# One decoder layer on one core: a gate projection is put in front of the SSD scan, the pieces between its half chunks get shorter, and the log gates of the GLA heads get PSUM banks of their own

## The chip, the cores and the metric

One core of a Trainium2 chip runs the whole program. The metric is the device time in microseconds (us); 3 runs of the kernel before are at hand, and one profiled execution.

## The reference

One layer of a decoder for 1024 prompt tokens and 8 samples of 8 tokens (1088 tokens), width 1024, all float32. h = RMSNorm(x) goes through one wide input projection `u = h @ W['w_in']`, whose columns feed three token mixers and the gates of each:

```python
g_log = log_sigmoid(g_low @ W['gla_w_alpha'] + W['gla_b_alpha']) / GLA_TAU      # log gates, 4 heads of 128
o, gla_s_new = gla_chunked(gq, gk, gv, g_log, gla_s)                            # GLA
y, ssd_h_new = ssd_chunked(sx, dt, a, sb, sc, ssd_h)                            # SSD, 16 heads, 2 groups
gates = sigmoid(gate_logits).reshape(b_, l_, 3, D_MODEL)
merged = gates[:, :, 0] * b_lru + gates[:, :, 1] * b_gla + gates[:, :, 2] * b_ssd
x = x + merged @ W['w_mix_out']
```

After it come cross attention and a SwiGLU.

## The kernel before

Activations lie transposed, features on the 128 partitions and tokens along the row. Every float32 product is made of three matmuls in a rounded format: high part by high part, high by low, low by high. A projection of one tile of 128 output features is 3 x 8 = 24 matmuls ("steps") for each of three groups of tokens (384, 384 and 320 columns, `GROUPS`), so 72 for a tile. SyncE loads a weight tile (512 KB) into one of three slots as soon as the tile that was there is used up; GpSimd splits it into Wh and Wl (L710, L712).

`plan()` writes down the order of all results in PSUM. Six banks form a ring, and a name in `OWN_BANK` has a fixed bank. Each bank has two counters: TensorE waits before its first matmul into a bank until the engine that reads the result before it there has let it go (`free_bank`), and a reader waits until the result is ready (`ready`). Each engine works its own list strictly in order.

Stages, in TensorE's order: LRU; four GLA heads; the `gla_out` product; the input projections of SSD (`sx`, `sz`) and their transposes (`st`, `zt`, L850); the SSD scan; the final states of the 8 samples; `ssd_out`; the mix; attention; the feed-forward.

**GLA heads.** `log_gates(h)` (L865) makes `ga{h}:0` to `:2` with one short product a group, ScalarE reads each twice (Abs L1717, Relu L1719), and then come the projections `gq`, `gk`, `gr`, `gv` of head h. For heads 1 to 3 the call stands at the end of the head before, just ahead of `turn_o(TT)`, the transposes of its last output, which wait until VectorE has scaled that output (L2493); it lies in bank 0 (`go{h}_8:0`). After those transposes VectorE multiplies (L2472), ScalarE copies two tiles (L1794), and only then reads `ga{h+1}`. For head 0 ScalarE comes to `ga0` when a store of the stage before has landed. All `ga` take their banks from the ring: 1, 2, 3 for head 0, then 0, 1, 2, then 5, 0, 1, then 4, 5, 0. The first projection `gq` takes 4, 5, 0 for head 0, then 3, 4, 5, then 2, 3, 4, then 1, 2, 3.

**SSD scan.** 8 chunks of 128 tokens by 2 head groups are 16 half chunks q. TensorE's list for one: `sums(q/2+1)` for even q, `products(q)` (L1146, L1149, L1153), the transposes `turn_y(q-1)` (L850), `fill(("q", q, 0))`, `decays(q+2)` (L1129), `fill(("q", q, 1))`. `fill` (L786) runs steps of the gate projections `og2_0` to `og2_7`, for which nobody in the scan waits. All `og2` results lie in bank 5. VectorE's list: `decay_steps(q+2)` (L2607), six operations of `outputs(q)` (L2634 to L2652), in even q `tile_sums`, then `matrices(q+2)` (L2616), `split_y(q-1)`, `scale_y(q)` (L2659). ScalarE's: in even q `exp_sums`, then `hi_y(q-1)` (L1958), `load_z`, `exp_decays(q+2)` (L1941), `load_xs`, `roots_y(q)` (L1950, L1951), and last `copy_gates_by_group(("q", q, 1))`: for each group of 24 steps that ends in that gap it copies bank 5 to a buffer (L1488) and stores it (L1490).

After the projections of SSD, and before it enters the scan, ScalarE waits for the stores of z, then issues the first loads (L1907, L1913); VectorE waits for the first of them, then makes `decay_steps(0)`. TensorE's first `decays(0)` waits for that.

**States.** For each of 8 samples: L1204, L850, L1211, L850, then `fill(("s", b))`. Then `decays` and `products` of the samples' own half chunks 16 and 17, `fill(("s", 8))`, `turn_y` of both, `fill(("s", 9))`. Behind the last gate copy ScalarE starts the loads of `ssd_out`.

Of the kernel before, what the change touches and what calls it, by code (L numbers as in the profile page):

```python
# [20 lines left out]
DT = D // P  # L21
LP = 1024
NB = 8
# [3 lines left out]
TT = LP // P  # L27
GROUPS = [(0, 384), (384, 384), (768, 320)]
# [3 lines left out]
GH, DK, DV, GCH = 4, 128, 256, 64  # L32
# [28 lines left out]
def gap_parts(b, tiles, gaps):  # L61


    parts, steps = {}, 3 * DT
    todo = [(t, g) for t in tiles for g in range(len(GROUPS))]
    at = 0
    for gap, n in gaps:
        parts[gap] = []
        while n:
            m = min(n, steps - at)  # L70
            parts[gap].append((f"og{b}_{todo[0][0]}", *todo[0], at, at + m))
            at, n = at + m, n - m
            if at == steps:
                at = 0
                todo.pop(0)
    assert not todo and at == 0
    return parts
# [3 lines left out]
GAPS = {}  # L81
# [7 lines left out]
OWN_BANK = {}  # L89
# [5 lines left out]
for _b in range(NB):  # L95
# [2 lines left out]
OWN_BANK |= {f"og2_{_t}:{_g}": 5 for _t in range(DT) for _g in range(len(GROUPS))}  # L98
OWN_BANK |= {f"og1_{_t}:{_g}": 4 + (_t * len(GROUPS) + _g) % 2 for _t in range(DT) for _g in range(len(GROUPS))}

GAPS |= gap_parts(2, range(DT), [(("q", _q, _i), 12) for _q in range(2 * TT) for _i in range(2)]
                  + [(("s", _b), 12) for _b in range(NB)] + [(("s", NB), 48), (("s", NB + 1), 48)])

# [4 lines left out]
def plan():  # L110
# [16 lines left out]
    def banks(name, n=len(GROUPS)):  # L127

        jobs.extend(f"{name}:{g}" for g in range(n))
# [66 lines left out]
    for t in range(DT):  # L196
        use([("in", C_Z + t * P)], f"sz{t}")
        banks(f"zt{t - 1}" if t else "qt")
    banks(f"zt{DT - 1}")
    banks("ss0", 2)  # L200
    banks("ss1", 2)
    for q in range(2 * TT):
# [9 lines left out]
    q = 2 * TT  # L212
# [53 lines left out]


WLIST, JOBS = plan()
RING = 6

# [16 lines left out]
def build(nc, ins, outs):  # L287
    I, O = ins, outs
    ctx = ExitStack()
    with ctx:  # L290
# [3 lines left out]
        def sem(name):  # L294
            return ctx.enter_context(nc.semaphore(name))
# [54 lines left out]
        def wk(i, n=WT, off=0):  # L350
            return WK[:, i * WT + off:i * WT + off + n]
# [20 lines left out]
        def EC(c):  # L372

            return wk(4, 32, D + 48 * (c % 2))
# [5 lines left out]
        def EL(c):  # L380

            return wk(4, 16, D + 96 + 16 * (c % 2)) if c < TT else wk(3, 128, D)

        def YZ(q):

            return wk(4, 512, q % 2 * 512)[0:P if q < 2 * TT else TS]
# [128 lines left out]
        def ready(eng, name):  # L515

            i, n = JOB[name]
            eng.wait_ge(ps_ready[i], n + 1)

        def read(eng, name):  # L520

            i, n = JOB[name]
            eng.wait_ge(ps_free[i], n + 1)
# [37 lines left out]
        def bank(name):  # L561
            return PS[:, JOB[name][0]]
# [4 lines left out]
        def freed(ins, name):  # L567
            ins.then_inc(ps_free[JOB[name][0]], 1)
# [4 lines left out]
        def S(name):  # L573
            if name not in sems:
                sems[name] = sem(name)
            return sems[name]
# [186 lines left out]
        def _(pe):  # L763
# [85 lines left out]
            def turn(out, in_, n):  # L849
                return pe.transpose(out, in_, ident[0:n, 0:n])  # L850
# [240 lines left out]
            def sums(c):  # L1091

                n = P if c < TT else TS
                cols = slice(c * P, c * P + n)
                le, gt = (m_le, m_gt) if c < TT else (s_le, s_gt)
                da = DTK[0:n, 1, c, :]
                if c == 0:
                    pe.wait_ge(S("s_act"), CT)
                    pe.wait_ge(S("dve_step"), STEP["dt_done"])
                    read(pe, f"st{CT - 2}:2")  # L1100
                else:
                    pe.wait_ge(S("sc_exp"), c)
                    pe.wait_ge(S("cbm"), c)

                def c_dot_b(g):
                    return pe.matmul(PM[0:n, 0, 160 + g * P:160 + g * P + n], bT[64 * g:64 * g + 64, cols],
                                     cT[64 * g:64 * g + 64, cols], start=True, stop=True)
                c_dot_b(0)
                pe.matmul(PM[0:n, 0, 0:16], le[:], da, start=True, stop=True)
                pe.matmul(PM[0:n, 0, 16:32], gt[:], da, start=True, stop=True)  # L1110
                if c < TT:
                    pe.matmul(PM[:, 0, 32:48], ones[:], da, start=True, stop=True).then_inc(S("cb0"), 1)
                else:
                    pe.wait_ge(S("dve_step"), STEP["dab"])
                    pe.matmul(PM[:, 0, 32:160], ones[0:n], DAB[0:n], start=True, stop=True)\
                        .then_inc(S("cb0"), 1)
                pe.wait_ge(S("cb0"), c + 1)
                c_dot_b(1).then_inc(S("sums"), 1)

            def decays(q):  # L1120

                n = P if q < 2 * TT else TS
                gt = m_gt if q < 2 * TT else s_gt
                name = f"ss{q}"
                pe.wait_ge(S("r"), q + 1)
                m = 512 // n
                for i in range(8 // m):
                    free_bank(pe, f"{name}:{i}")
                    done(pe.matmul(bank(f"{name}:{i}")[0:n].rearrange("p (h i) -> p h i", i=n), gt[:],  # L1129
                                   RM(q)[:, i * m:(i + 1) * m], start=True, stop=True), f"{name}:{i}")  # L1130
# [26 lines left out]
            def turn_y(q):  # L1157
                n = P if q < 2 * TT else TS
                pe.wait_ge(S("y_norm"), q + 1)
                if q:  # L1160
                    pe.wait_ge(S("sy_lo"), q)
                for k in range(4):
                    mm = turn(PM[:, 1, k * P:k * P + n], YZ(q)[:, k * P:(k + 1) * P], n)
                mm.then_inc(S("y_turned"), 1)
            sums(0)
            decays(0)
            decays(1)
# [53 lines left out]
            q = 2 * TT  # L1221
# [231 lines left out]
        def _(act):  # L1453
# [24 lines left out]
            def copy_gates_by_group(gap):  # L1478

                for name, t, g, first, end in GAPS[gap]:  # L1480
                    if end < 3 * DT:
                        continue
                    t0, n = GROUPS[g]
                    j = 3 * t + g
                    if j >= 2:
                        act.wait_ge(S(f"m_put{j % 2}"), 16 * (GATE_PUTS[2] + j // 2))
                    ready(act, f"{name}:{g}")
                    freed(act.activation(SG[:, j % 2, 0:n], bank(f"{name}:{g}")[:, 0:n], ACT.Copy), f"{name}:{g}")  # L1488
                    read(act, f"{name}:{g}")
                    act.dma_start(gates[1, t][:, t0:t0 + n], SG[:, j % 2, 0:n]).then_inc(S(f"m_put{j % 2}"), 16)  # L1490
# [215 lines left out]
            for h in range(GH):  # L1706
# [56 lines left out]
                for c in range(TT + 1):  # L1763
                    n = P if c < TT else TS
                    q = h * (TT + 1) + c
# [136 lines left out]
            def load_z(q):  # L1902
                c, g = divmod(q, 2)
                n = P if c < TT else TS
                if q >= 2:
                    act.wait_ge(S("y_turned"), q - 1)
                act.dma_start(YZ(q), z_scr[c * P:c * P + n, g * 512:(g + 1) * 512]).then_inc(S(f"z_in{q % 2}"), 16)  # L1907

            def load_xs(q):
                c, g = divmod(q, 2)  # L1910
                n = P if c < TT else TS
                half = slice(g * 512, (g + 1) * 512)
                act.dma_start(wk(3)[0:n, half], x_scr[c * P:c * P + n, half]).then_inc(S(f"xs_in{g}"), 16)  # L1913
# [14 lines left out]
            def exp_sums(c):  # L1928
                n = P if c < TT else TS
                m = 16 if c < TT else 128  # L1930
                act.wait_ge(S("sums"), c + 1)
                act.activation(EC(c)[0:n], PM[0:n, 0, 0:32], ACT.Exp)
                act.activation(EL(c), PM[:, 0, 32:32 + m], ACT.Exp).then_inc(S("sc_exp"), 1)

            def exp_decays(q):
                n = P if q < 2 * TT else TS
                name = f"ss{q}"
                m = 512 // n
                for i in range(8 // m):
                    ready(act, f"{name}:{i}")  # L1940
                    freed(act.activation(RM(q)[:, i * m:(i + 1) * m],  # L1941
                                         bank(f"{name}:{i}")[0:n].rearrange("p (h i) -> p h i", i=n), ACT.Exp),
                          f"{name}:{i}")
# [18 lines left out]
            load_z(1)  # L1962
            load_xs(0)
            load_xs(1)
            exp_sums(0)
            exp_decays(0)
            exp_decays(1)
            for q in range(2 * TT):
                if q % 2 == 0:
                    exp_sums(q // 2 + 1)  # L1970
                if q:
                    hi_y(q - 1)
                    load_z(q + 1)
                if q + 2 < 2 * TT:
                    exp_decays(q + 2)
                act.wait_ge(S("x_used"), q + 1)
                load_xs(q + 2)
                roots_y(q)
                copy_gates_by_group(("q", q, 1))
# [36 lines left out]
            q = 2 * TT  # L2016
# [180 lines left out]
            for c in range(FC):  # L2197
                for i in range(2):
                    q = 2 * c + i
# [749 lines left out]
```

## Time and profile before

| | |
|---|---|
| median of 3 runs | 3043.49 us (3043.2 to 3043.82) |
| profiled execution | 3039.03 us, span of the core 3037.3 us |
| TensorE busy | 2914.4 us (96%) |
| VectorE, ScalarE, GpSimd busy | 1238.3, 680.1, 855.9 us |
| mean granted TensorE clock | 0.983 |

The span runs from the first to the last instruction. [...] A matmul's row gives its start and its duration; consecutive ones overlap, so the time of many is read from the chain, which counts only from one start to the next.

### The profile page before, as it was taken

The numbers are of one execution on the slowest core, as the hardware profiler recorded it, in microseconds if no ns is written. First come the engines' busy times: TensorE is split into PE (matmuls) and PEld (weight loads), VectorE is DVE, ScalarE is ACT, GpSimd is POOL, SyncE is SP. The second block draws the span as 40 slices with busy tenths as digits, with TensorE's granted clock in tenths as the row PEclk, the third lists the DMA queues.
The fourth block names the chain that finished last, engine by engine and source line by source line (L and its number), as shares of the span: only waits on it lengthen the run. The fifth ranks groups of instructions, "written<-read, shape, count | busy, mean of one in ns | idle before, by whom it ended". The sixth has DMA issues, their size and how long they took to land.

```text
span 3037.3 us, 41522 instructions
## 1 busy us (share of the span) xinstructions
PE 2914.4 (96%) x17736; PEld 2735.6 (90%) x17736; DVE 1238.3 (41%) x1893; ACT 680.1 (22%) x1233; POOL 855.9 (28%) x509
## 2 busy tenths in 40 slices
PE   7999999999999999989987999998999999999998
PEld 6998999797988899987756999987999999999998
DVE  5886102324232247517853211325153333333335
ACT  3554001123121112225533122124020000000001
POOL 3232232111211223223421443301232323323221
PEclk9999999999999999999998999999999999999999
DMA  3111222212121533232232433143111111111112
GB/s 112 42 35 38 71 64 62 68 34 70 45 67 34 166 128 86 73 94 69 79 100 96 149 88 105 49 146 119 35 49 48 44 42 49 42 45 47 42 49 73
DMA packets 300389, 216.88 MB, mean 71 GB/s; under 512 B 30762, under 2 KB 279659, under 8 KB 300208
## 3 DMA queue, kind: packets, MB, share of 16 engines
q1 hardware_dynamic: 226832, 136.67, 15.8%
q10 hardware_dynamic: 73376, 77.57, 7.8%
q8 instruction: 141, 2.31, 0.3%
q14 instruction: 40, 0.33, 0.0%
HBM read 173.48 MB, written 40.73 MB: 71 GB/s over the span
## 4 chain that ended last, share of the span: by engine, by line
PE 88%; DVE 6%; ACT 2%; issue 1%; DMA 1%; SPq 1%; ACTq 0%; POOL 0%; DVEq 0%
PE PS L770 53%; PE PS L1416 9%; PE PS L786 6%; PE PS L842 3%; DVE WK L2231 3%; PE PS L850 2%; PE PS L810 2%; PE PS L828 1%; PE PS L865 1%; PE PS L1153 1%; PE PS L1129 1%; PE PS L1296 1%; PE PS L1320 1%; PE PM L997 1%; PE PS L1013 1%
## 5 line engine op out<-in xcount | busy, mean ns | idle before, releaser
L770 PE MATMUL PS<-Hh,Wh 128*128 128x384 f32 (+1 forms) x2928 | 965.3, 330 | 5.4 <-POOL Wl L712 4.0
L770 PE MATMUL PS<-Hh,Wl 128*128 128x384 f32 (+1 forms) x2928 | 959.9, 328 | 0.0
L770 PE MATMUL PS<-Hl,Wh 128*128 128x384 f32 (+1 forms) x2928 | 959.4, 328 | 0.0
L710 POOL CAST Wh<-Wr 128x1024 fp32r<-128x1024 f32 x213 | 248.5, 1166 | 1959.9 <-DMA Wr<-in_w_in 811.0
L770 PEld LDWEIGHTS PS<-Hh,Wh 128*128 128x128 f32 x2928 | 553.3, 189 | 7.3 <-POOL Wl L712 4.2
L770 PEld LDWEIGHTS PS<-Hl,Wh 128*128 128x128 f32 x2928 | 553.3, 189 | 0.6
L770 PEld LDWEIGHTS PS<-Hh,Wl 128*128 128x128 f32 x2928 | 552.9, 189 | 0.0
L712 POOL TENSOR_TENSOR Wl<-Wr,Wh 128x1024 fp32r<-128x1024 f32 x213 | 537.4, 2523 | 17.1
L2231 DVE SCALAR_TENSOR_TENSOR WK<-WK,PS 128x384 f32<-128x384 f32 x186 | 98.4, 532 | 606.9 <-PE PS L770 444.6
L770 PE MATMUL PS<-Yh,Wh 128*128 128x384 f32 (+1 forms) x576 | 190.7, 331 | 8.8 <-DVE Yl L2534 4.8
L2859 DVE TENSOR_TENSOR X<-X,PS 128x384 f32<-128x384 f32 (+1 forms) x264 | 135.8, 531 | 154.2 <-PE PS L1416 77.2
L770 PE MATMUL PS<-Yh,Wl 128*128 128x384 f32 (+1 forms) x576 | 190.2, 330 | 0.0
L770 PE MATMUL PS<-Yl,Wh 128*128 128x384 f32 (+1 forms) x576 | 190.2, 330 | 0.0
L1416 PE MATMUL PS<-Fh,Wh 128*128 128x384 f32 (+1 forms) x528 | 173.4, 328 | 3.6 <-DVE KVh L2231 3.6
L1416 PE MATMUL PS<-Fh,Wl 128*128 128x384 f32 (+1 forms) x528 | 173.2, 328 | 0.0
L1416 PE MATMUL PS<-Fl,Wh 128*128 128x384 f32 (+1 forms) x528 | 172.8, 327 | 0.0
L786 PE MATMUL PS<-Hh,Wh 128*128 128x384 f32 (+1 forms) x384 | 137.3, 357 | 1.4 <-ACT SG L1488 1.4
L786 PE MATMUL PS<-Hh,Wl 128*128 128x384 f32 (+1 forms) x384 | 129.0, 336 | 0.0
L786 PE MATMUL PS<-Hl,Wh 128*128 128x384 f32 (+1 forms) x384 | 129.0, 336 | 0.0
L770 PEld LDWEIGHTS PS<-Yh,Wh 128*128 128x128 f32 x576 | 110.1, 191 | 9.3 <-DVE Yl L2534 5.0
L2205 ACT ACTIVATE WK<-WK 128x1088 f32<-128x1088 f32 x22 | 24.5, 1115 | 407.8 <-DVE WK L2879 407.7
L2231 DVE SCALAR_TENSOR_TENSOR WK<-WK 128x1088 f32<-128x1088 f32 (+1 forms) x78 | 96.5, 1241 | 45.4 <-ACT WK L2205 29.3
(419 smaller groups left out, 4101.9 us busy)
## 6 DMA issues: line engine op xcount, KB each, us to landing
Wr<-in_w_in SPq DMA_DIRECT2D x82, 512.0 KB, 3.8
Wr<-in_w_ffn_gate SPq DMA_DIRECT2D x22, 512.0 KB, 3.7
Wr<-in_w_ffn_up SPq DMA_DIRECT2D x22, 512.0 KB, 3.7
Wr<-in_w_ffn_down SPq DMA_DIRECT2D x22, 512.0 KB, 3.7
merged<-WK ACTq DMA_DIRECT2D x16, 544.0 KB, 4.0
WK<-gates ACTq DMA_DIRECT2D x16, 544.0 KB, 4.9
WK<-merged ACTq DMA_DIRECT2D x16, 544.0 KB, 6.0
Wr<-in_w_lru_out SPq DMA_DIRECT2D x8, 512.0 KB, 4.6
```

The costliest lines, as they stand in the source:

```text
L710: pool.tensor_copy(Wh[:, n % SLOTS], Wr[:, n % SLOTS]).then_inc(w_hi, 1)
L712: pool.tensor_tensor(Wl[:, n % SLOTS], Wr[:, n % SLOTS], Wh[:, n % SLOTS].bitcast(F32), ALU.subtract).then_inc(w_split, 1)
L770: mm = pe.matmul(bank(f"{name}:{g}")[:, 0:n], L[:, w % SLOTS, k, :], R[:, k, t0:t0 + n], start=(k == 0 and i == 0), stop=(last and k == DT ...
L786: mm = pe.matmul(bank(f"{name}:{g}")[:, 0:n], L[:, w % SLOTS, s // 3, :], R[:, s // 3, t0:t0 + n], start=(s == 0), stop=(s == 3 * DT - 1), ...
L810: mm = pe.matmul(bank(f"{name}:{g}")[:, 0:n], L[:, (w + j) % SLOTS, k, :], R[:, k, t0:t0 + n], start=(k == 0 and i == 0), stop=(k == DT - ...
L828: mm = pe.matmul(bank(name)[:, 0:M], L[:, w % SLOTS, k, :], R[:, k, :], start=(k == 0 and i == 0), stop=(k == DT - 1 and i == 2))
L842: mm = pe.matmul(bank(f"{name}:{c // 2}")[0:n, (c % 2) * 256:(c % 2) * 256 + 256] .rearrange("p (a m) -> p a m", a=2), A[:, k, c * P:c * P ...
L850: return pe.transpose(out, in_, ident[0:n, 0:n])
L865: done(pe.matmul(bank(f"{name}:{g}")[:, 0:n], lhsT, rhs[:, t0:t0 + n], start=True, stop=True), f"{name}:{g}")
L1416: mm = pe.matmul(bank(f"{name}:{g}")[:, 0:n], lhsT, R[:, e % 2, k, t0:t0 + n], start=(k == 0 and i == 0), stop=(k == 1 and i == 2))
L2231: return dve.scalar_tensor_tensor(out=out, in0=in0, scalar=scalar, in1=in1, op0=op0, op1=op1)
L2859: freed(dve.tensor_tensor(X[:, t, t0:t0 + n], X[:, t, t0:t0 + n], bank(f"{name}:{g}")[:, 0:n], ADD), f"{name}:{g}")
```

## The change

A new gap `("q", -1, 0)` of 72 steps, the whole tile `og2_0`, stands in front of `sums(0)`; ScalarE's copies of its three groups stand behind its four first loads of the scan, ahead of `exp_sums(0)`. Each of the 32 gaps between half chunks gets 10 steps for 12, each of the 8 of the states 13 for 12, and the last two 40 for 48. A group's 24 steps no longer end at the end of a gap: within the scan one group ends and the next begins inside the gaps (q, 0) of half chunks 1, 2, 7, 8, 13, 14 and (q, 1) of 3, 4, 9, 10, 15. ScalarE gets a call for the gaps (q, 0) as well, between `load_z` and `exp_decays(q+2)`. The `ga` results leave the ring for banks 1, 2 and 4. By the order in `plan()` this moves other results on the ring: `gq` now takes 1, 2, 3 for head 0, 3, 4, 5 for head 1, 5, 0, 1 for head 2 and 1, 2, 3 for head 3. The order of the weight tiles does not change.

```diff
-GAPS |= gap_parts(2, range(DT), [(("q", _q, _i), 12) for _q in range(2 * TT) for _i in range(2)]
-                  + [(("s", _b), 12) for _b in range(NB)] + [(("s", NB), 48), (("s", NB + 1), 48)])
+GAPS |= gap_parts(2, range(DT), [(("q", -1, 0), 72)] + [(("q", _q, _i), 10) for _q in range(2 * TT) for _i in range(2)]
+                  + [(("s", _b), 13) for _b in range(NB)] + [(("s", NB), 40), (("s", NB + 1), 40)])
+
+OWN_BANK |= {f"ga{_h}:{_g}": (1, 2, 4)[_g] for _h in range(GH) for _g in range(len(GROUPS))}
...
     banks(f"zt{DT - 1}")
+    gap(("q", -1, 0))
     banks("ss0", 2)
...
+            fill(("q", -1, 0))
             sums(0)
             decays(0)
...
             load_xs(1)
+            copy_gates_by_group(("q", -1, 0))
             exp_sums(0)
...
                     load_z(q + 1)
+                copy_gates_by_group(("q", q, 0))
                 if q + 2 < 2 * TT:
```

## Rows read from the trace of the kernel before

**Rows 1.** Windows: stretch, us, busy of each engine, granted clock, DMA share, GB/s.
```profile
1371.01:1536.44 165.43, 163.90 (x866) 120.09 (x866) 137.32 (x229) 92.61 (x189) 65.31 (x52) 1.00 0.25 78
...
603.70:613.70 10.00, 9.56 (x24) 7.38 (x25) 3.08 (x4) 4.83 (x8) 3.38 (x2) 0.50 0.17 65
743.40:746.80 3.40, 3.40 (x13) 3.28 (x12) 1.76 (x3) 2.62 (x4) 1.82 (x1) 0.50 0.00 0
876.50:883.20 6.70, 6.70 (x21) 5.86 (x20) 2.95 (x3) 5.03 (x9) 2.95 (x2) 0.50 0.15 52
```

**Rows 2.** Timeline, TensorE, heads' ends: start, us, line, idle before and releaser.
```profile
604.14 3.96 PE L865 MATMUL PS<-WK,CB 16*128 16x384 f32 x6 [2.40 <-DVE YA L2493]
...
741.97 1.45 PE L865 MATMUL PS<-WK,CB 16*128 16x384 f32 x4 [1.64 <-DVE YA L2493]
...
876.16 1.13 PE L865 MATMUL PS<-WK,CB 16*128 16x320 f32 x2 [0.88 <-DVE YA L2493]
877.22 0.47 PE L850 MATMUL PM<-ident,YA 64*128 64x64 f32 x2
```

**Rows 3.** Timeline, heads 0 and 3: log gates and ScalarE's reads.
```profile
471.08 2.09 PE L865 MATMUL PS<-WK,CB 16*128 16x384 f32 x6
...
476.76 0.57 ACT L1719 ACTIVATE YA<-PS,LAM 128x384 f32<-128x384 f32 x1
...
880.55 0.57 ACT L1719 ACTIVATE YA<-PS,LAM 128x384 f32<-128x384 f32 x1
```

**Rows 4.** Timeline, all engines, from the SSD projections into the scan.
```profile
1358.16 0.83 ACTq L1907 DMA_DIRECT2D WK<-z_scr  x2
...
1360.01 0.20 ACT L1932 ACTIVATE WK<-PM 128x32 f32<-128x32 f32 x1 [5.53 <-issue]
...
1363.73 3.78 PE L1129 MATMUL PS<-Ylf,m_gt 128*128 128x512 f32 x4 [9.49 <-DVE Ylf L2607]
1363.90 2.29 POOL L734 TENSOR_TENSOR Yhf<-WK 128x512 f32<-128x512 f32 x1 [6.28 <-DVE WK L2597]
...
1366.15 1.03 POOL L739 TENSOR_TENSOR Yhf<-WK 128x512 f32<-128x512 f32 x1
```

**Rows 5.** Chain that ended last, half chunks 2 and 3: start, us, what.
```profile
1397.24 1.76 PE PS L786 x12
1399.00 1.72 PE PS L1129 x4
...
1406.46 0.45 PE PM L850 x4
1406.90 2.09 PE PS L786 x12
```

**Rows 6.** Timeline, ScalarE, gate copies of half chunks 3 and 9, reads after 0.
```profile
1414.49 0.47 ACT L1488 ACTIVATE SG<-PS 128x384 f32<-128x384 f32 x1
...
1480.58 0.47 ACT L1488 ACTIVATE SG<-PS 128x384 f32<-128x384 f32 x1
...
1385.70 0.88 ACT L1958 ACTIVATE Yh<-PM,PV 128x128 fp32r<-128x128 f32 x3
```

**Rows 7.** Waits inside 1350 to 1530: who for whom, us, times, longest.
```profile
DVE Ylf L2607 <- PE PS L1153: 15.8, 7, 2.9
...
DVE WK L2607 <- PE PS L1153: 6.4, 5, 2.0
...
PE PM L850 <- DVE WK L2659: 1.1, 2, 0.6
```

**Rows 8.** Chain that ended last, from the states to the last gap.
```profile
1593.99 0.02 issue
...
1597.22 1.98 PE PS L1129 x2
...
1612.16 0.45 ACT SG L1488
...
1612.74 4.42 PE PS L786 x24
```

## The prediction

> **What bounds the kernel now.** I read the windows by stage first, then the chain of waits, then the timeline at each place that the diff touches. In the scan, from the first `products` to the last, TensorE is busy 163.90 of 165.43 us [rows 1], so each step taken out there is time gained, and each wait put in there is time lost. VectorE is busy 137.32 us; it waits before `decay_steps` for TensorE, 15.8 + 6.4 us in 12 of 16 half chunks [rows 7], so it is not the bound and would hardly become it when 3.3 steps in 20 less are waited for. Ahead of the scan TensorE idles 9.49 us, since VectorE waits for the first load of z [rows 4]. At the ends of the heads it idles 2.40, 1.64 and 0.88 us, for `scale_o` [rows 2]. So there are two places to win, and the question is what the new order makes TensorE wait for.
>
> **Head ends (the ga banks).** Four entries, one by one.
>
> Head 0: `gq0:0` now lies in bank 1, right behind `ga0:0`. TensorE is through with `ga0` at 471.08 + 2.09 = 473.17, but ScalarE's second read of the first group ends at 476.76 + 0.57 = 477.33 [rows 3]. Before, `gq0` went into other banks. A new wait of 4.2 us. After such an idle time the clock falls: stretches at 0.50 that follow the three idle times of rows 2 last 10.0, 3.4 and 6.7 us [rows 1]. I take the shortest here, which costs half of 3.4, 1.7. Together +5.9.
>
> Head 1: the six `ga` matmuls took 3.96 us, at half clock, after the wait for `go0_8:0` [rows 2]. In banks 1, 2, 4 nothing holds them, they run inside the idle time, at the full clock in about 2 us. `turn_o` then comes 3.96 us sooner. `gq1:1` in bank 4 must wait for ScalarE's read of `ga1:2`, some 1.3 us. The time after the turn at half clock, 613.7 - 608.5 = 5.2 us and so 2.6 lost, is mostly spared. Together -3.96 + 1.3 - 2.6 = -5.2. Head 2: four matmuls, 1.45 us [rows 2], leave the path; the low stretch of 3.4 us costs 1.7 and may or may not stay, half taken: -2.3.
>
> Head 3: two matmuls leave the path, which brings the last turn 1.1 us forward (877.22 to about 876.1, its end to 876.6) [rows 2]. But `gq3:0` now lies in bank 1 behind `ga3:0`. ScalarE's second read of that ended at 881.12 [rows 3], 3.4 us behind the turn's end (877.70), and it follows the turn at the same distance: next start at 880.0, with a low stretch of at least 3.4 us behind it, 881.7 in all-high terms. Before it was 877.70 plus half of the 5.5 us to 883.2, so 880.45. +1.3.
>
> Sum of the heads: 5.9 - 5.2 - 2.3 + 1.3 = -0.3 (bounds -3 and +3 by how the clock falls).
>
> **In front of the scan.** 72 steps are 2 x 24 x 0.174 + 24 x 0.147 = 11.9 us (2.09 and 1.76 for 12 [rows 5]). They can start at 1352.5. `og2_0:0` ends at 1356.6. `og2_0:1` needs the same bank 5, and ScalarE comes to the copy only behind its store waits and four load issues, where `exp_sums(0)` stood: 1360.01 [rows 4]. So TensorE waits 4 us for 1360.5 and is at half clock for some 3.4 us of what follows. Group 1 ends at 1366.2, group 2 (copy 0.47 and hand over 0.15 between) at 1370.4. `sums(0)` took 1.8 us: 1372.2. Only then come `exp_sums(0)`, VectorE's `wj`, GpSimd's L734 and L739, 2.29 + 1.03 us [rows 4], which XDT needs, and beside them the decays, ScalarE's exp and a matrices of 2.1 us. `products(0)` starts at 1376.9 by that; it started at 1371.0. +5.9 (4.3 if the clock stays, 8 if it is late twice). What hides 6 of the 11.9 us is the idle time of 9.49; `products(0)` is what is late next, and nobody else is hurt.
>
> **In the loop.** To the last `products` 15 half chunks have 4 steps less: 60 x 0.165 = -9.9; TensorE's waits for `scale_y` [rows 7] go too: -1.1.
>
> Against that, bank 5 is handed over inside gaps. For (q, 1) take q = 3 with rows of before. `products(3)` ended at 1406.46 [rows 5]. TensorE reaches the hand over after turn 0.45, 10 steps 1.74, decays 1.72 and 2 steps 0.3: at 4.2 us. ScalarE copies only behind `roots_y(3)`, which follows VectorE's whole `outputs(3)`: the copy ends at 1414.49 + 0.47 = 1414.96, at 8.5 us [rows 6]. A wait of 4.3 us on TensorE, with `products(4)`, `turn_y(3)` and all behind it in its queue. q = 9 ends its products at 1472.1 and its copy at 1481.05 [rows 6]: 4.5. q = 4 and 10 have 6 steps ahead of the hand over and, pushed away from GpSimd's weight split by the wait before them, a quicker VectorE: 2.8 and 2.9. q = 15 lies behind the last `products`, where TensorE had to wait for `scale_y(15)` anyway: 0. Sum 14.5.
>
> For (q, 0) ScalarE does `hi_y` first: 1385.70 + 0.88 = 1386.6 [rows 6], then copies in 0.5, 2.0 us after the turn ended. TensorE has 4 steps, 0.7 us, to run in q = 1, 7, 13 (wait 1.3), 8 steps in q = 2, 8, 14 (0.6, 0.6, 0.8). Sum 5.9.
>
> The clock: four waits of 2.8 to 4.5 us are longer than the three idle times after which it fell [rows 1, 2]. Each costs between half of 3.4 and half of 10.0, so 1.7 and 5.0; I take 2.5, near the short end, since gate steps run right after: +10. For the waits near 1 us I take nothing (each 0 to 1.7: 0.88 us was enough at head 3).
>
> [...]
>
> Loop: -9.9 - 1.1 + 14.5 + 5.9 + 10 = +19.4.
>
> **States and tail.** 8 steps more: +1.3. Hand overs within the gaps of samples 1, 3, 4, 6 behind a copy of 0.6 us: 0.7 each, +2.9. Since no group ends with sample 7, ScalarE does not copy it ahead of the samples' sums: `decays(16)` waited from 1593.99 to 1597.22 [rows 8], -3.0. In the gap after sample 8's products ScalarE goes on once 32 steps are done, for 48 before: -2.6. The last gap has 8 less: -1.3. Sum -2.7 (bounds -5 and 0).
>
> **The sum.** -0.3 + 5.9 + 19.4 - 2.7 = +22.3 on the profiled execution's 3039.03, so 3061.3. The median of the runs stands 4.5 above that execution, so it's 3065.8.
>
> **The rivals.**
>
> *The clock forgives.* The long waits in the loop let it fall by chance late, or not at all: 10 less, 3056. For it: the copies are gone before gate steps at full width. Against: three idle times, three falls. 0.2.
>
> *Hand overs are cheap.* Where a hand over is awaited already, as at 1612.16 to 1612.74, TensorE lost 0.66 us [rows 8]. If each of the ten in the loop cost this, because ScalarE is ahead of where I put it, the loop is -9.9 - 1.1 + 6.6 = -4.4 with no fall of the clock, the front +2, and the whole -0.3 + 2 - 4.4 - 2.7 = -5.4, with the heads' bound -8: 3036, faster. It decides from a mean wait of 0.7 us downward; mine is 2.0. Against it stands ScalarE's strict order, in which `roots_y` must be over. 0.06; halfway, within 0.2% (3037.4 to 3049.6, about what a measurement here tells from no change): 0.06.
>
> *The clock never recovers in the loop.* Each of the ten waits brings a low stretch of 6.7 us, 3.4 lost: 34 for 10, so 3090. For it: 0.88 us of idle was enough once, and the busy stretch 603.7 to 613.7 stayed low for 10 us [rows 1]. [...] 0.13.
>
> *My forecast*, a net loss with four waits of 3 to 4.5 us: 0.55. Its own range is 3058 to 3075.
>
> **Range.** Low end: no clock in the loop (-10), front 4.3 (-1.6), heads -3: 3051. High end: 5 us per long wait (+10), 1.7 for three short ones (+5), heads +3: 3084. That leaves the cheap hand overs and most of the third rival out. Chances: faster 0.06, within 0.2% 0.07, slower 0.87.
>
> **What would show it.** After the change TensorE L786 waits for ScalarE SG L1488 some 28 us in all, the longest 4 us; TensorE L770 waits about 4.2 and 3.4 us for ScalarE L1719 at heads 0 and 3; L865 no longer waits for L2493; the first `products` starts 6 us later and the last 25 us later; the loop's granted clock is some 0.88 to 0.93. Wrong I am if the loop's waits for SG sum to under 10 us, or if its clock stays at 1.00.

## Result: slower by 1.5%, twice what was forecast

The changed kernel takes 3090.6 us (median of 4, 3088.39 to 3091.63), the kernel before 3043.65 beside it: a ratio of 1.0153, 95% interval 1.0136 to 1.0171. The forecast was 3065.8 with a range to 3084, so the sign was right and the time lies above the range. The profiled execution took 3090.31 us, 51.3 more than that of before.

I read the windows by stage first. Columns are as in [rows 1]; the first row is the scan's loop from the first `products` to the last, then four stretches inside it and one at head 3.

```profile
1385.04:1579.23 194.19, 174.86 (x785) 123.46 (x784) 127.78 (x225) 89.65 (x183) 65.13 (x53) 0.87 0.20 59
1428.00:1445.00 17.00, 14.99 (x47) 11.14 (x48) 4.21 (x10) 4.48 (x10) 6.58 (x5) 0.50 0.12 38
1452.00:1462.40 10.40, 10.40 (x33) 7.15 (x32) 2.59 (x4) 1.78 (x5) 1.81 (x2) 0.51 0.10 31
1513.40:1527.00 13.60, 13.54 (x47) 9.76 (x46) 2.87 (x4) 2.04 (x7) 4.61 (x4) 0.50 0.09 27
1533.50:1544.00 10.50, 10.50 (x34) 7.74 (x35) 3.49 (x5) 2.42 (x5) 1.70 (x2) 0.52 0.12 40
...
878.80:888.60 9.80, 5.02 (x16) 5.05 (x17) 2.82 (x3) 8.08 (x11) 2.94 (x2) 0.50 0.09 32
```

The same span of work took 161.34 us before (1371.01 to 1532.35, the start of the last `products`) at a granted clock of 1.00 [rows 1]; now it takes 194.19 at 0.87. The loop alone has grown by 32.85 us, with 60 matmuls less in it. I put the clock's loss at 13% of the 194.19 us, 25.2 us, an estimate from the granted clock of 0.87. The four stretches say the same: 51.5 us at 0.50, half of it lost. At 1.00 a gate step of 384 columns starts 0.17 us behind the one before it (1532.92 to 1533.09), at 0.50 0.32 us (1541.35 to 1541.67).

The waits of TensorE, first in the whole execution, then (the last row) from 1381 to 1600: who for whom, us, times, longest.

```profile
PE PS L789 <- ACT SG L1492: 32.4, 20, 4.7
PE PS L773 <- ACT YA L1723: 10.6, 3, 4.9
...
PE PS L789 <- ACT SG L1492: 22.4, 11, 4.7
```

L789 is the gate step in `fill`, L1492 ScalarE's copy of a finished group. Before, TensorE waited for that copy twice, 1.4 us in all; now 20 times. L773 (a head's first projection) waiting for L1723 (ScalarE's second read of the log gates) is new too.

TensorE's timeline at those waits, heads 0, 1 and 3, then the front, then half chunks 3, 4, 9 and 10:

```profile
477.83 0.66 PE L773 MATMUL PS<-Hh,Wh 128*128 128x384 f32 x1 [4.39 <-ACT YA L1723]
...
610.98 0.33 PE L853 MATMUL PM<-ident,YA 64*128 64x64 f32 x2 [0.23 <-DVE YA L2499]
...
883.58 0.66 PE L773 MATMUL PS<-Hh,Wh 128*128 128x384 f32 x1 [4.93 <-ACT YA L1723]
...
1366.61 0.56 PE L789 MATMUL PS<-Hh,Wh 128*128 128x384 f32 x1 [3.96 <-ACT SG L1492]
...
1429.95 0.66 PE L789 MATMUL PS<-Hh,Wh 128*128 128x384 f32 x1 [4.71 <-ACT SG L1492]
...
1451.25 0.41 PE L789 MATMUL PS<-Hh,Wh 128*128 128x384 f32 x1 [2.33 <-ACT SG L1492]
...
1512.50 0.39 PE L789 MATMUL PS<-Hh,Wh 128*128 128x320 f32 x1 [4.12 <-ACT SG L1492]
...
1532.49 0.41 PE L789 MATMUL PS<-Hh,Wh 128*128 128x384 f32 x1 [2.44 <-ACT SG L1492]
```

Each of the last four waits stands at the edge of one of the four low stretches. Only in the first does the clock fall while TensorE still waits (1428.3, the wait ends at 1429.95). In the other three it falls 0.8, 1.0 and 1.5 us after TensorE is at work again, when most or all of the 4 or 8 gate steps that follow the wait in its gap have run at full clock. For the second:

```profile
1451.50:1452.00 0.50, 0.50 (x4) 0.37 (x3) 0.37 (x1) 0.00 (x0) 0.50 (x2) 1.00 0.06 22
1452.00:1452.50 0.50, 0.50 (x3) 0.37 (x2) 0.00 (x0) 0.00 (x0) 0.50 (x1) 0.54 0.96 350
```

The other six waits in the loop up to the last `products` take 0.68 to 1.07 us, 5.2 in all, and no low stretch follows them.

Why the wait is so long is seen in ScalarE's timeline in half chunk 3. The group was ready at 1425.24; the copy (L1492) stands behind the two roots (L1954, L1955), and these behind VectorE:

```profile
1427.15 0.63 ACT L1954 ACTIVATE YT<-WK 128x512 f32<-128x512 f32 x1 [1.57 <-DVE WK L2658]
1427.68 0.19 ACT L1954 ACTIVATION_READ_ACCUMULATOR YT<-WK 128x1 f32 x1
1427.89 1.28 ACT L1955 ACT_TABLE_LOAD   x1
1429.18 0.29 ACT L1955 ACTIVATE ST<-ST,EPSC 128x1 f32<-128x1 f32 x1
1429.39 0.42 ACT L1492 ACTIVATE SG<-PS 128x320 f32<-128x320 f32 x1
```

Of TensorE's 4.71 us, 1.28 go to the table that ScalarE loads ahead of the second root (ACT_TABLE_LOAD).

Where the 51.3 us are, by the start of the same instruction in both profiles: +5.95 at the end of the last z projection (heads), +8.1 from there to `products(0)` (front), +32.85 to `products(15)` (loop), +4.4 behind it. Of these 4.4, 1.2 are there when the SSD output projection starts (1638.13 before, 1686.25 now); the other 3.2 come behind its start, in code that the diff leaves alone.

### The profile page after: what moved, and what is told of

It reads as the page before. It is cut to its first block, busy times and chain, and to the rows that moved or that the text cites. A ratio compares the mean times of both kernels' runs of the same rounds, so it can differ in the third digit from the quotient of the medians.

```text
span 3088.6 us, 41522 instructions
## 1 busy us (share of the span) xinstructions
PE 2943.6 (95%) x17736; PEld 2757.0 (89%) x17736; DVE 1230.9 (40%) x1893; ACT 680.6 (22%) x1233; POOL 851.8 (28%) x509
## 4 chain that ended last, share of the span: by engine, by line
PE 87%; DVE 5%; ACT 3%; issue 1%; DMA 1%; SPq 1%; ACTq 0%; POOL 0%; DVEq 0%
PE PS L773 52%; PE PS L1420 8%; PE PS L789 6%; PE PS L845 3%; DVE WK L2237 2%; PE PS L853 2%; PE PS L813 2%; PE PS L831 1%; PE PS L1156 1%; PE PS L1300 1%; PE PS L868 1%; PE PS L1132 1%; PE PS L1324 1%; PE PM L1000 1%; PE PS L1152 1%
## 5 line engine op out<-in xcount | busy, mean ns | idle before, releaser
L773 PE MATMUL PS<-Hh,Wh 128*128 128x384 f32 (+1 forms) x2928 | 964.5, 329 | 15.9 <-ACT YA L1723 10.6
L773 PE MATMUL PS<-Hh,Wl 128*128 128x384 f32 (+1 forms) x2928 | 958.9, 327 | 0.0
L773 PE MATMUL PS<-Hl,Wh 128*128 128x384 f32 (+1 forms) x2928 | 958.6, 327 | 0.0
L773 PEld LDWEIGHTS PS<-Hh,Wh 128*128 128x128 f32 x2928 | 553.4, 189 | 18.2 <-issue 11.5
L773 PEld LDWEIGHTS PS<-Hl,Wh 128*128 128x128 f32 x2928 | 553.3, 189 | 0.6
L773 PEld LDWEIGHTS PS<-Hh,Wl 128*128 128x128 f32 x2928 | 553.0, 189 | 0.0
L773 PE MATMUL PS<-Yh,Wh 128*128 128x384 f32 (+1 forms) x576 | 190.0, 330 | 8.8 <-DVE Yl L2540 4.8
L773 PE MATMUL PS<-Yl,Wh 128*128 128x384 f32 (+1 forms) x576 | 189.5, 329 | 0.0
L773 PE MATMUL PS<-Yh,Wl 128*128 128x384 f32 (+1 forms) x576 | 189.3, 329 | 0.0
L789 PE MATMUL PS<-Hh,Wh 128*128 128x384 f32 (+1 forms) x384 | 137.8, 359 | 32.4 <-ACT SG L1492 32.4
L789 PE MATMUL PS<-Hl,Wh 128*128 128x384 f32 (+1 forms) x384 | 136.5, 355 | 0.0
L789 PE MATMUL PS<-Hh,Wl 128*128 128x384 f32 (+1 forms) x384 | 135.6, 353 | 0.0
L773 PEld LDWEIGHTS PS<-Yh,Wh 128*128 128x128 f32 x576 | 109.6, 190 | 9.3 <-DVE Yl L2540 5.0
L789 PEld LDWEIGHTS PS<-Hh,Wh 128*128 128x128 f32 x384 | 77.0, 200 | 42.6 <-issue 41.8
L853 PEld LDWEIGHTS PS<-ident,WK 128*128 128x128 f32 (+6 forms) x432 | 55.6, 163 | 66.1 <-DVE WK L2237 19.1
```

What stands on the lines that cost most here:

```text
L773: mm = pe.matmul(bank(f"{name}:{g}")[:, 0:n], L[:, w % SLOTS, k, :], R[:, k, t0:t0 + n], start=(k == 0 and i == 0), stop=(last and k == DT ...
L789: mm = pe.matmul(bank(f"{name}:{g}")[:, 0:n], L[:, w % SLOTS, s // 3, :], R[:, s // 3, t0:t0 + n], start=(s == 0), stop=(s == 3 * DT - 1), ...
```

## The experiments

The theory: the loop loses by the waits at hand-overs of bank 5 inside a gap and, more, by the low clock behind the long ones. Rivals: the wait alone is the price; the ten short waits bring the clock down as well (the prediction's third rival); or the front and the banks put the engines out of step. Each time stands beside the kernel before on the same chip, whose single executions spread from 3035.3 to 3051.2 us; the medians of the variants are over 4 to 12 executions. Profiles are of one execution each.

**The two halves apart.** The first kernel is before plus the `ga` line, the second is the changed one without it.

> The kernel before with the banks of the log gates alone (ga in banks 1, 2, 4); the gaps stay as they were. What the trace of after suggests: TensorE waits for ScalarE's second read of ga at heads 0 and 3 (about 4.4 and 4.9 us), heads 1 and 2 gain 3.4 and 1.4 us, and the low clock behind the two waits costs the rest, so the whole is 5 to 6 us over before, 3048.6 to 3049.6. Rival, the prediction's own sum of the heads: -0.3, no difference from before. What tells them apart: the start of the head after each head end, and how long the granted clock stays at 0.50 behind the waits.

> The changed kernel without the banks of the log gates: the new gaps and the two new copies alone. If the heads cost 5 to 6 us and the rest is independent of them, 3090.6 - 5.5 = 3085. If instead the long low stretches in the loop depend on what the heads did to the clock earlier, the loop loses less than the 33 us that it lost in the changed kernel.

Measured: the banks alone 3050.16 (before 3044.91; ratio 1.0017, 1.0005 to 1.0029), the gaps alone 3087.24 (1.0137, 1.0117 to 1.0157). +5.2 and +42.3 make 47.5, for 47.0 of the whole change: the two add up. The banks alone show the same two waits for ScalarE at the heads, 4.51 and 4.83 us, and the gaps alone the same four in the loop, 4.71, 2.33, 4.09 and 2.45. Their loop is as long and has as low a clock:

```profile
1378.72:1572.90 194.18, 174.80 (x785) 123.50 (x784) 129.30 (x225) 89.78 (x183) 64.97 (x53) 0.87 0.19 59
```

So this pattern is no accident of one execution. It isn't fixed either: the five executions of the gaps alone go from 3074.14 to 3092.33. The banks of the log gates are a loss, not the small gain of my sum.

**The copy ahead of the roots.** The gaps alone, with ScalarE's copy moved:

```diff
+                copy_gates_by_group(("q", q, 1))
                 act.wait_ge(S("x_used"), q + 1)
                 load_xs(q + 2)
                 roots_y(q)
-                copy_gates_by_group(("q", q, 1))
```

> The change's gaps (log gates as before), with ScalarE's copy of the groups that end in gap (q, 1) moved ahead of its waits for VectorE's use of x, the load of xs and the roots. The hand-over of bank 5 stays inside the gap, but the copy should run as soon as the group ends. Theory (TensorE waits 2.3 to 4.7 us since ScalarE stands behind the roots, and the low clock follows those four waits): the four waits shrink to some 0.7 us each, 13.6 to 2.8, and with them 25 us of low clock go: about 35 us less than the kernel with the gaps alone, some 3050. Rival A (any hand-over inside a gap lets the clock fall, however short): only the 11 us of waits go, some 3074. Rival B (ScalarE is then late with the roots, which VectorE and TensorE wait for later): no gain.

Measured: 3054.23 (before 3044.91; 1.0030, 1.0019 to 1.0041), 33.0 less than the gaps alone. The loop's window and the waits of 1381 to 1600:

```profile
1374.81:1536.88 162.07, 152.90 (x785) 107.55 (x784) 135.97 (x225) 90.77 (x183) 71.09 (x53) 1.00 0.24 70
```

```profile
PE PS L788 <- ACT SG L1491: 12.2, 15, 1.1
```

There are as many hand-overs inside the gaps as before this edit; none brings a wait longer than 1.1 us, and the clock stays at 1.00 for the whole loop. So these short waits don't bring it down (rival A, and the prediction's third rival, fall), and what ScalarE now does later costs little (TensorE waits for `scale_y` 1.8 us in two places, most of it behind the last `products`), so rival B falls. By the profiles the loop gives back 32.1 us, of which the shorter waits are about a third.

**Work in place of the idle time.** This separates the clock from the wait: TensorE isn't served sooner, it only has something to do.

```diff
                     if end == 3 * DT:
+                        if gap[0] == "q":
+                            for _ in range({(3, 1): 22, (4, 1): 9, (9, 1): 22, (10, 1): 9}.get(gap[1:], 0)):
+                                mm = pe.matmul(..., start=False, stop=True, ...)
                         done(mm, f"{name}:{g}")
```

> The change's gaps with the log gates as before (3087 us on the chip of its run), and TensorE kept at work where it would wait in gaps (3,1), (4,1), (9,1) and (10,1): the last step of the group that ends there is done 22, 9, 22 and 9 times more, 3.8 and 1.6 us of matmuls in place of as much idle time. This adds the last product to these four groups' gates again and again, so that part of the output is another; no data or order changes otherwise. Theory (the idle time lets the clock fall, and 25 us of the loop's loss are matmuls at 0.50): the waits shrink by what the extra steps take, the clock stays at 1.00, and the whole is some 25 us less, about 3062. Rival (the loop's loss beyond the waits comes from something else, such as VectorE and ScalarE out of step): no gain, 3085 or more.

Measured: 3073.32 (before 3045.42; 1.0094, 1.0081 to 1.0107), 14 less than the gaps alone, where I expected 25. The loop's window, and the four places in TensorE's timeline:

```profile
1379.92:1558.01 178.09, 166.91 (x847) 120.26 (x846) 128.30 (x225) 90.17 (x183) 64.84 (x53) 0.97 0.22 64
```

```profile
1424.64 0.41 PE L788 MATMUL PS<-Hh,Wh 128*128 128x384 f32 x1 [1.49 <-ACT SG L1495]
...
1439.63 0.41 PE L788 MATMUL PS<-Hh,Wh 128*128 128x384 f32 x1 [1.34 <-ACT SG L1495]
...
1496.54 0.39 PE L788 MATMUL PS<-Hh,Wh 128*128 128x320 f32 x1 [0.73 <-ACT SG L1495]
...
1511.25 0.41 PE L788 MATMUL PS<-Hh,Wh 128*128 128x384 f32 x1 [2.00 <-ACT SG L1495]
```

The 62 extra matmuls take 9.9 us and shorten the waits by 8.0; the clock's loss falls from 25.2 to 5.3 (3% of 178). That is -18.0, and the loop is 16.1 us shorter. Three of the four low stretches are gone. The one that is left, 1512 to 1522, follows the wait of 2.00 us. So the 25 us were the clock's, and it was the idle time that let it fall. The rest of my expectation failed by one low stretch of 10 us that stayed, and by 2 us of added work that covered no wait.

**One wait alone, in the kernel before.**

```diff
+_STEPS = {(3, 0): 22, (3, 1): 10, (4, 0): 4}
-GAPS |= gap_parts(2, range(DT), [(("q", _q, _i), 12) for _q in range(2 * TT) for _i in range(2)]
+GAPS |= gap_parts(2, range(DT), [(("q", _q, _i), _STEPS.get((_q, _i), 12)) for _q in range(2 * TT) for _i in range(2)]
```

> The kernel before with one hand-over of bank 5 put inside a gap: gaps (3,0), (3,1) and (4,0) get 22, 10 and 4 steps in place of 12 each, so that a group ends two steps into gap (3,1), in front of ScalarE's roots of half chunk 3. One wait of about 2.6 us (TensorE gets there 12 steps later than in the changed kernel, whose wait was 4.7). Theory (a wait of 2.3 us or more brings a low stretch of 10 us or more, 5 us lost): +7.5 over before. The prediction's term (2.5 for the clock): +5. Rival (the wait alone): +2.6.

Measured: 3048.06 (before 3045.42; 1.0013, 1.0004 to 1.0022), +2.6 by the medians and +4.0 by the ratio. My theory's 7.5 is excluded (its 1.0025 lies outside the interval); the time alone doesn't tell the prediction's +5 from the rival's +2.6, so the profile has to. TensorE's timeline at the wait, and the windows of the loop and of its only low stretch:

```profile
1414.16 0.66 PE L787 MATMUL PS<-Hh,Wh 128*128 128x384 f32 x1 [3.02 <-ACT SG L1489]
```

```profile
1369.32:1534.23 164.91, 161.32 (x844) 118.50 (x843) 129.97 (x220) 90.10 (x184) 65.90 (x52) 0.99 0.25 74
1414.00:1417.40 3.40, 3.24 (x10) 2.83 (x10) 0.83 (x2) 1.29 (x2) 3.32 (x4) 0.51 0.16 58
```

Here the wait of 3.02 us brought 3.4 us at 0.50, a loss of 1.7, and not the 10 us or more that I expected; less the 1.1 us for which TensorE no longer waits for `scale_y`, that is the 3.6 us by which the loop grew. The wait alone is not the whole price, then, but the clock's part is small. The length of the low stretch doesn't follow the length of the wait: behind 2.00, 2.33, 2.44, 3.02, 4.12 and 4.71 us it was 10, 10.4, 10.5, 3.4, 13.6 and 17.0 us. What the profiles do show is where it ended. In the changed kernel all four ended inside or right behind the ten gate steps that follow the next turn (1445.3, 1462.4, 1527.1, 1544.2), after a whole `products` and turn had gone by at 0.50; here the clock fell inside the wait (1414.0), and the stretch ended behind the eight gate steps that follow it. That doesn't explain all: at half chunk 3 of the changed kernel it fell inside the wait as well, and eight such steps didn't end it.

**Gaps whose ends are the groups' ends.** The changed kernel without the `ga` line, and:

```diff
-GAPS |= gap_parts(2, range(DT), [(("q", -1, 0), 72)] + [(("q", _q, _i), 10) ...]
-                  + [(("s", _b), 13) for _b in range(NB)] + [(("s", NB), 40), (("s", NB + 1), 40)])
+GAPS |= gap_parts(2, range(DT), [(("q", -1, 0), 72)] + [(("q", _q, _i), 12) ...]
+                  + [(("s", _b), 12) for _b in range(NB)] + [(("s", NB), 24), (("s", NB + 1), 0)])
```

> The gaps of the change laid so that no group of the gate projection ends inside a gap of the loop: 72 steps in front, 12 in each half chunk's two gaps and in each of the seven samples' gaps, 24 and 0 at the end; log gates as before. The edit moves steps and leaves the computation whole. Theory (waits at hand-overs inside the gaps, and the low clock behind them, are the loop's loss): no wait of TensorE for the gate copies in the loop, granted clock of the loop 1.00, the loop no longer than before. The front costs some 8 us, the end has 72 steps less (11.9 us): about 3040, 3036 to 3044. Rival (work put in front of the scan, or other banks in use, shifts the whole loop out of step with VectorE and ScalarE): the loop stays 15 us or more longer than before, over 3055.

(There are eight samples' gaps, not seven; the steps are as in the diff.) Measured: 3036.29 (before 3044.91; 0.9978, 0.9967 to 0.9988). The loop's window:

```profile
1380.27:1541.53 161.26, 159.76 (x845) 117.47 (x844) 131.69 (x220) 90.24 (x184) 67.84 (x53) 1.00 0.25 76
```

161.26 us for 161.34 before, at a clock of 1.00: the loop is untouched, though the front, the extra copies and the 72 steps ahead are there. Nothing is out of step; that rival falls. The front costs as much as in the changed kernel: 28.81 us from the last z projection to `products(0)` for 28.83, and 20.75 before. The kernel is faster than before all the same since these 72 steps, 11.9 us of matmuls, are missing behind the loop.

**The front.** Two steps on top of the even gaps. First the order alone:

```diff
-            fill(("q", -1, 0))
             sums(0)
+            fill(("q", -1, 0))
...
-            copy_gates_by_group(("q", -1, 0))
             exp_sums(0)
+            copy_gates_by_group(("q", -1, 0))
```

then three banks as well: `OWN_BANK |= {"og2_0:1": 0, "og2_0:2": 1}`.

> The even gaps with only the order of the front changed: the first chunk's sums ahead of the 72 steps on TensorE and their exp ahead of the gate copies on ScalarE, all three groups still in bank 5. It tells what of the front's 9 us is the sums that came late, and what the waits for bank 5. Theory (both count: the first products are held by the chain from the sums to the weighted x, which then runs beside the steps): most of the gain of the front in three banks, products starting 2 to 4 us later than there, 3031 to 3034. Rival (the waits for bank 5 are the cost, since ScalarE is now even later with the copies): at most 2 us under the even gaps, 3034 to 3036.

> The even gaps (72, 12 each, 24, 0) with a front that waits for nothing: the first projection's second and third group in banks 0 and 1 in place of 5, the first chunk's sums ahead of it on TensorE, and ScalarE's exp of them ahead of the gate copies. The computation is whole. Theory (the front costs 8 to 9 us by the wait for bank 5, the low clock behind it and the sums that come late): the first products start within 2 us of before, and the whole is some 7 us under the even gaps alone, about 12 us under before, 3031. Rival (72 steps don't fit in front: TensorE has 9.5 us idle there and the steps take 11.9, and the new banks 0 and 1 make others wait): at most 3 us under the even gaps.

Measured: order alone 3032.34 (before 3043.44; 0.9967, 0.9955 to 0.9979), with the banks 3029.77 (before 3045.42; 0.9952, 0.9940 to 0.9965). The front takes 26.03 us with the order, 21.11 with both, for 20.75 before and 28.8 in the even gaps. TensorE's waits in the front of the first, and the copies in the second, where no step waits:

```profile
1360.37 0.66 PE L788 MATMUL PS<-Hh,Wh 128*128 128x384 f32 x1 [2.21 <-ACT SG L1491]
...
1367.00 0.38 PE L788 MATMUL PS<-Hh,Wh 128*128 128x320 f32 x1 [0.67 <-ACT SG L1491]
```

```profile
1358.54 0.50 ACT L1493 ACTIVATE SG<-PS 128x384 f32<-128x384 f32 x1
...
1361.12 0.49 ACT L1493 ACTIVATE SG<-PS 128x384 f32<-128x384 f32 x1 [2.08 <-PE PS L790]
...
1364.44 1.88 PE L1133 MATMUL PS<-Ylf,m_gt 128*128 128x512 f32 x4
```

So of the front's 8.1 us the order gives back 2.8 and the banks 4.9. I had expected most from the order; it is the smaller part, and the waits for bank 5 the larger. The 72 steps (11.9 us) then fit in the hole in front of the scan for 0.4 us. In the changed kernel this hole hid 3.8 of the 11.9 us, not the 6 of the prediction; with the order and the banks changed it hides nearly all.

**The log gates in other banks.** Before, with banks that neither the head's last output nor the next head's first group of q holds; the line in `OWN_BANK` alone would shift every later tile, so the ring still counts them.

```diff
+OWN_BANK |= {f"ga{_h}:{_g}": ((1, 2, 3), (1, 2, 5), (4, 1, 5), (4, 5, 0))[_h][_g] for _h in range(GH) for _g in range(len(GROUPS))}
...
-    if _name not in OWN_BANK:
+    if _name not in OWN_BANK or _name.startswith("ga"):
```

> The kernel before with banks of their own for the log gates, chosen so that they are neither the bank which the head's last output still holds nor that of the next head's first group of q, and with all other tiles left in the banks they had. If the change's loss at heads 0 and 3 comes from q's first group lying in the bank of the log gates that ScalarE still reads, it is gone here, and heads 1 and 2 keep their gain of 3.4 and 1.4 us and head 3 gains about 1: 4 to 6 us under before, 3039 to 3041. Rival (a late log gate was hidden by the later turn, so nothing is won): within 1 us of before.

Measured: 3038.14 (before 3045.42; 0.9977, 0.9966 to 0.9989). From 460 to 950 us TensorE waits no more for the log gates' reads, and for `scale_o` 1.4 us in three places (before 4.9 for L865 alone); who for whom, us, times, longest:

```profile
PE PS L867 <- DVE YA L2495: 0.8, 1, 0.8
PE PM L852 <- DVE YA L2495: 0.6, 2, 0.4
```

Log gates that run inside the idle time at the heads' ends are worth 7 us (3 to 10 by the interval), if the next tile isn't put behind them.

**The samples' gaps alone**, in the kernel before: 13 steps for 12 in each of the eight, 44 and 44 for 48 and 48.

> The kernel before with the change's 13 steps in each of the samples' gaps in place of 12, and 44 and 44 in place of 48 and 48 at the end: hand-overs of bank 5 inside the samples' gaps, the half chunks untouched. The prediction put the samples and the end, with 8 steps more, at -2.7; the changed kernel's profile shows +2.1 there. With the steps' number kept, the prediction's terms give -3.0 -1.8 +2.9 = some -2; the profile's reading gives 0 to +2.

Measured: 3044.95 (before 3043.44; 1.0002, 0.9993 to 1.0010): no difference that shows; of a gain of 2 us, only the very end of the interval is left. `decays(16)` in TensorE's timeline waits less but starts later than in [rows 8]. ScalarE's line ahead of it:

```profile
1595.67 0.49 ACT L1488 ACTIVATE SG<-PS 128x384 f32<-128x384 f32 x1 [0.34 <-PE PS L786]
...
1598.82 1.92 PE L1129 MATMUL PS<-Ylf,s_gt 64*64 64x512 f32 x2 [1.11 <-ACT WK L2015]
```

That is 67.7 us behind the last `products`, and was 64.9. But this run is no test of the -3.0 for `decays(16)`: the loop has 384 steps here, so a group ends five steps into sample 7's gap (384 + 7 x 13 + 5 = 480, twenty groups of 24), and ScalarE still copies it ahead of the samples' sums. What it tests is the four hand-overs and the 8 steps ahead: by the profile they cost 4.0 us, for 4.2 of the prediction (2.9 and 1.3).

**Both repairs together**, and the same with the last 24 steps in the other of the two last gaps.

> Both repairs together: the even gaps with the front in three banks (14 to 16 us under before alone) and the log gates in banks of their own with the other tiles' banks kept (7 us under before alone). The computation is whole. If the two act at different places, they add up: 21 to 23 us under before, some 3023. Rival (a head end that comes earlier meets another late transfer, or the first products are held by the load of z): 16 us or less.

> The same as the kernel with both repairs, with the 24 gate steps that are left for the end in the very last gap and none in the one ahead of it (0 and 24 in place of 24 and 0). If the last gap is where TensorE would otherwise idle with a low clock, 1 to 4 us less than with both repairs; if the gap behind sample 8's products is that place, 1 to 4 us more.

Measured: 3020.81 (before 3043.44; 0.9932, 0.9920 to 0.9944) and 3022.37 (0.9935, 0.9923 to 0.9948). The repairs add up, -22.6 for -15.7 (even gaps with the front in three banks) and -7.3. The place of the last 24 steps makes no difference that shows. The kernel with both repairs is 22.6 us faster than before and some 70 faster than the change as it was made, with the same work. Span and clock of its core:

```profile
core 0: 3017.2 us, clock 0.986
```

## Why the prediction was wrong

**What bounds the kernel** was right: each wait put into the loop came out at the end.

**Hand-overs in the loop: right.** The long waits were 4.71, 2.33, 4.12 and 2.44 (13.6) for 4.3, 2.8, 4.5 and 2.9 (14.5); the six short ones 5.2 for 5.9; q = 15 had no effect on the last `products`, as said (for what came behind it, see the end). The removed steps (-9.9) and the wait for `scale_y` (-1.1) stand. With 18.8 of waits and 25.2 of clock the sum is 33.0, for 32.85 measured.

**The clock in the loop: the step that failed.** It said "Each costs between half of 3.4 and half of 10.0, so 1.7 and 5.0; I take 2.5, near the short end, since gate steps run right after: +10." The four cost 8.5, 5.2, 6.8 and 5.3 (half of each stretch), 25 in all. Two things were wrong. The bounds came from heads' ends, where long projections follow; in the loop only 4 or 8 gate steps follow, then (at half chunks 3 and 9) the next chunk's sums, `products` and a turn. In three of the four the gate steps were through, or nearly so, before the clock fell, and so were no help; and `products` and the turn went at 0.50 in all four. And the short end was taken where nothing spoke for it: one low stretch as short as that was found, in the kernel with one wait, and there the low stretch ended behind the gate steps as I had thought. Rows of before had a hint: at head 2 the wait ended at 741.97 and the stretch at 0.50 began at 743.4, after four matmuls [rows 1, 2]. That the idle time is the cause is shown by the copy moved ahead and by the work put in place of the idle time. What makes one stretch 3 us and another 17 is open.

**The heads: wrong in sum, by 6.2 (+5.95 for -0.3).** By the start of each head's v projection: head 0 +6.9 (5.9 said), head 1 -3.4 (-5.2), head 2 -1.5 (-2.3), head 3 +3.6 (+1.3). At head 3 I had ScalarE's second read follow the turn at the old distance. But the turn that came sooner did not bring it: ScalarE first waited 2.82 us for the store of the last state before it could write `Yh`:

```profile
880.39 2.11 ACT L1798 ACTIVATE Yh<-WK 128x1088 fp32r<-128x1088 f32 x2 [2.82 <-DMA out_s_gla_S<-YA]
...
882.87 0.57 ACT L1723 ACTIVATE YA<-PS,LAM 128x384 f32<-128x384 f32 x1
```

So the new wait was 4.93 us, and 9.8 us around it were at 0.50.

**The front: nearly right**, 8.1 for 5.9 (bound 8). The wait was 3.96 us, as said.

**Samples and end: wrong by 7** (+4.4 for -2.7). The terms that it named came out nearly as said. The four hand-overs in samples' gaps cost 3.15 us for 2.9. `decays(16)` starts 3.5 us behind the start of the last sample's last transposes, for 6.0 before, since no copy stands ahead of it: -2.5 for -3.0. From there to the SSD output projection 3.2 us are gained for 3.9. What it put at nothing is the clock behind the wait of q = 15. TensorE waits 3.61 us there, and the low stretch that begins in this wait is longer than the one in the same place before (first row before, second now; the third is `decays(16)` now):

```profile
1545.60:1555.70 10.10, 6.32 (x18) 2.37 (x19) 6.95 (x12) 2.33 (x6) 4.68 (x3) 0.50 0.42 97
...
1588.80:1605.60 16.80, 13.29 (x42) 8.94 (x43) 7.68 (x16) 3.92 (x10) 6.40 (x5) 0.50 0.39 95
...
1648.55 1.07 PE L1132 MATMUL PS<-Ylf,s_gt 64*64 64x512 f32 x2 [0.93 <-ACT WK L2021]
```

At sample 1's first product, ahead of any hand-over in the samples' gaps, 1.9 us are lost. The last 3.2 us of the 4.4 come behind the start of the output projection, in code that wasn't touched; a single execution can't say more of them.

The difference of 29.0 between 3061.3 and the profiled 3090.31 is then 13.5 in the loop (15.2 of clock, less 1.7 of waits), 6.2 at the heads, 2.2 in front and 7.1 behind. With the clock in the loop right, the forecast would have been 3081, within the range to 3084; it was the largest error, not the only one.

**The rivals.** The third gave the measured time, 3090, by a mechanism that the runs exclude: ten waits with a low stretch of 6.7 us each. It was four with 10 to 17. In the changed kernel the loop's clock is 0.87; with the copy ahead of the roots there are as many idle times at the same bank, of 0.7 to 1.1 us, and the clock is 1.00. So a hand-over awaited at each group didn't bring it down by itself; in the loops it fell only at waits of 2.0 us or more. "The clock forgives" and "hand overs are cheap" fell for the kernel as changed, the second because of ScalarE's order alone: with the copy ahead of the roots, the hand-overs in the loop cost 0.7 to 1.1 us, near the 0.66 that it took.

## What to carry to other kernels

Give back a PSUM bank where the engine that reads it is free, or let groups end where the gap ends: one copy queued behind another engine's chain cost 14 us in waits and 25 in clock, and one line moved gave back 33 of the whole. In the scan's loops the waits of 2.00 to 4.71 us were followed by 3.4 to 17.0 us at 0.50: when a new wait of such a length stands ahead of a stage of small matmuls, bound the clock's loss by that whole stage at half clock, not by the shortest low stretch seen elsewhere (3.4 us here). Before a tile is put in a bank, look at who uses that bank next and when its last reader gets there: `gq`, put behind the log gates' reads, waited 4.39 and 4.93 us.

## What was not expected of the hardware

- In the scan ten waits of up to 1.1 us, and two of 1.34 and 1.49 us, left the clock at 1.00, while at a head's end of the changed kernel a low stretch of 3.4 us began at 612.4, behind small matmuls, a wait of 0.23 us, a turn and six matmuls of the next projection. Idle time alone doesn't tell when the clock falls.

```profile
612.40:615.80 3.40, 3.40 (x12) 3.40 (x12) 0.98 (x1) 2.12 (x3) 2.18 (x1) 0.50 0.04 9
```

- The fall came, in three of the loop's four, after the engine was at work again: behind the wait that ended at 1512.50 six gate steps ran at full clock, and 0.50 began at 1513.5; behind the one that ended at 1532.49 it began at 1534.0. The steps had run by then, and `products(10)` went at half speed: the 16 matmuls of its last line (L1156) took 3.68 us, for 2.00 before.
- Over whole executions of the kernel before, with the same instructions, the time spread by some 16 us (3035.3 to 3051.2): a difference of a few us needs medians.
